# A two-block transformer kernel on one core: other reading places for the modulation sums, later gates, vectors turned in one go

## What is computed

```python
# first block
f = swiglu(rmsnorm(x, ffn1_pre_g), w_gate, w_up, w_down); x = x + 0.5*rmsnorm(f, ffn1_post_g)
# mixer: one projection h @ w_in is split into q, k, v of 12 attention heads,
#   q, k, v, o of 4 mLSTM heads, 4 + 4 gate columns (i_pre, f_pre) and two branch gates
ig = i_pre + i_bias;  lf = log_sigmoid(f_pre + f_bias)      # mLSTM gates, per head and token
att = dilated_window_attention(...);  hm = mlstm_chunkwise(q, k, v, ig, lf)
merged = sigmoid(g_a)*(att @ w_att_branch) + sigmoid(g_m)*(ml @ w_mlstm_branch)
x = x + rmsnorm(merged @ w_out, mix_post_g)
x = x + 0.5*rmsnorm(swiglu(...), ffn2_post_g)
# second block, two layers (i = 0: sparse attention, i = 1: short convolution)
mod = silu(c) @ ada_w[i] + ada_b[i]                          # 1024 -> 6144, one row
sh1, sc1, g1, sh2, sc2, g2 = split(mod, 6)
h = rmsnorm(x, norm1_g[i])*(1 + sc1) + sh1;  x = x + g1*mixer_i(h)
h = rmsnorm(x, norm2_g[i])*(1 + sc2) + sh2;  x = x + g2*swiglu(h, ...)
```

## Time and profile before

| | |
|---|---|
| median of three runs | 2851.05 us |
| the profiled execution, its own time | 2849.39 us |
| its span | 2847.6 us |
| PE busy | 2756.6 us, 97% of the span |
| DVE, ACT, POOL busy | 48%, 33%, 29% |
| mean granted PE clock | 0.97 of full speed |

### The profile page before, as it was taken

One profiled execution on the slowest core, in us unless ns is written; L12 is line 12 of the kernel. 1 busy time (PEld: TensorE's weight loads), 2 busy tenths in 40 slices (PEclk: granted clock), 3 DMA queues, 4 the chain that ended last, 5 costly groups with the idle time before them and its releaser, 6 DMA issues.

```text
span 2847.6 us, 30406 instructions
## 1 busy us (share of the span) xinstructions
PE 2756.6 (97%) x12474; PEld 2174.6 (76%) x12474; DVE 1359.3 (48%) x1932; ACT 936.6 (33%) x1528; POOL 813.4 (29%) x683
## 2 busy tenths in 40 slices
PE   7999998999999989999999987999999999999999
PEld 6788886777777768888888654468888888888887
DVE  4343255545665534544424697564333454633323
ACT  4222243333444322432224423443222232332221
POOL 5563024443654487457300233410000000000000
PEclk9999999999999999999999996699999999999999
DMA  5453243333333255344433211022333423333332
GB/s 168 141 148 121 97 114 107 101 95 87 110 104 104 82 144 163 115 134 148 119 126 101 62 45 44 9 67 67 96 97 133 126 59 96 126 97 96 96 111 82
DMA packets 380765, 294.52 MB, mean 103 GB/s; under 512 B 14805, under 2 KB 334545, under 8 KB 380625
## 3 DMA queue, kind: packets, MB, share of 16 engines
q1 hardware_dynamic: 363632, 240.33, 28.4%
q0 software_dynamic: 16992, 52.25, 6.1%
HBM read 290.40 MB, written 2.13 MB: 103 GB/s over the span
## 4 chain that ended last, share of the span: by engine, by line
PE 84%; DVE 9%; ACT 3%; POOL 2%; DMA 1%; issue 1%; SPq 0%; DVEq 0%; ACTq 0%; POOLq 0%
PE PS L342 17%; PE PS L343 16%; PE PS L345 14%; PE PS L408 7%; PE PS L410 7%; PE PS L409 7%; PE PS L347 2%; PE PS L839 2%; PE PS L379 1%; PE PS L380 1%; PE PS L381 1%; PE PS L860 1%; DVE SCW L2076 1%; DVE M L2073 1%; PE PS L849 1%; DVE WL L1474 1%
## 5 line engine op out<-in xcount | busy, mean ns | idle before, releaser
L342 PE MATMUL PS<-HH,WH 128*128 128x512 f32 x2248 | 906.6, 403 | 0.0
L343 PE MATMUL PS<-HL,WH 128*128 128x512 f32 x2248 | 878.6, 391 | 0.0
L345 PE MATMUL PS<-HH,WL 128*128 128x512 f32 x1967 | 769.7, 391 | 0.0
L1474 DVE TENSOR_TENSOR WL<-RAW,WH 128x1024 fp32r<-128x1024 f32 (+1 forms) x306 | 400.9, 1312 | 546.1 <-ACT WH L899 545.9
L342 PEld LDWEIGHTS PS<-HH,WH 128*128 128x128 f32 x2248 | 424.6, 189 | 131.2 <-issue 47.5
L343 PEld LDWEIGHTS PS<-HL,WH 128*128 128x128 f32 x2248 | 424.5, 189 | 90.8 <-issue 6.8
L899 ACT ACTIVATE WH<-RAW 128x1024 fp32r<-128x1024 f32 (+1 forms) x318 | 330.5, 1041 | 377.4 <-PE PS L347 312.5
L345 PEld LDWEIGHTS PS<-HH,WL 128*128 128x128 f32 x1967 | 371.0, 189 | 79.4
L2248 POOL TENSOR_SCALAR ADA<-ADA,CA 128x512 f32<-128x512 f32 x168 | 294.7, 1754 | 12.5 <-DMA ADA<-in_ada_w 5.0
L2245 POOL TENSOR_TENSOR ASUM<-ASUM,ADA 128x512 f32<-128x512 f32 x168 | 230.4, 1372 | 14.0
L1474 DVE TENSOR_TENSOR WLr<-RAWD,WHr 128x1024 fp32r<-128x1024 f32 x82 | 101.7, 1240 | 257.4 <-ACT WHr L899 257.4
(11 more groups left out here) (327 smaller groups left out, 3468.4 us busy)
## 6 DMA issues: line engine op xcount, KB each, us to landing
ADA<-in_ada_w POOLq DMA_DIRECT2D x192, 256.0 KB, 3.2
RAW<-in_ffn_w_gate SPq DMA_DIRECT2D x88, 512.0 KB, 3.9
RAW<-in_ffn_w_up SPq DMA_DIRECT2D x88, 512.0 KB, 3.9
RAWD<-in_ffn_w_down SPq DMA_DIRECT2D x88, 512.0 KB, 3.4
RAW<-in_w_in SPq DMA_DIRECT2D x84, 512.0 KB, 3.9
RAW<-in_conv_w_in SPq DMA_DIRECT2D x24, 512.0 KB, 3.9
RAW<-in_attn_w_in SPq DMA_DIRECT2D x16, 512.0 KB, 3.8
RAW<-in_w_mlstm_branch SPq DMA_DIRECT2D x8, 512.0 KB, 4.0
```

What stands on the lines that cost most here:

```text
L342: pe.matmul(PS[:, b, :], wh[:, k, :], hi[:, k, :], start=k == 0, stop=False)
L343: pe.matmul(PS[:, b, :], wh[:, k, :], lo[:, k, :], start=False, stop=False)
L345: pe.matmul(PS[:, b, :], wl[:, k, :], hi[:, k, :], start=False, stop=False)
L1474: return v.tensor_tensor(out, x, y, op).then_inc(*tick("dve", *event))
```

## The change

Three edits. The list `FLUSH` still holds 24 chunks; its first 15 are the same (up to chunk 135). Before, entries 15 to 18 were chunks 142, 149, 156 and 163, and 19 to 23 were 178, 185, 192, 199 and 206. Now entries 15 to 17 are 144, 153 and 160, and 18 to 23 are 178, 185, 192, 199, 206 and 213. On all three engines `gates()` is appended when chunk `MIX` + 4 (the fifth of the mixer) has been handled, and not stepped at once. The three later groups of vectors are turned by three transposes in a row and copied by one instruction.

```diff
-FLUSH = (list(range(F1 + 8, F1 + 40, 7)) + list(range(MIX + 6, BR2 + 13, 7)) + list(range(F2 + 3, F2 + 40, 7)))[:24]
+FLUSH = (list(range(F1 + 8, F1 + 40, 7)) + list(range(MIX + 6, BR1 + 1, 7)) + [BR1 + 9, BR2 + 2, BR2 + 9]
+         + list(range(F2 + 3, F2 + 40, 7)))
...
 # tensor_program
     def later_vectors():
         for g in range(1, 4):
-            turn_vectors(g)
+            w.wait_ge(*at("vs", g))
+        for g in range(1, 4):
+            c0, n = SIZES[g]
+            ins = pe.transpose(PS[:, 7, c0:c0 + n], m["VS"][0:n, g, :], C[0:n, C_ID:C_ID + n])
+        ins.then_inc(*tick("pe", "vt", 3))
+        free[7] = ("vec", 3)
...
                 i = MIX + 1 + 9 * hd + 3 * g + which
                 if i >= at_i["chunk"]:
                     fm(h, side_bank())
+                if i == MIX + 4:
+                    behind.work.append(gates())
...
     head(1, [4, 0, 1])
     w.wait_ge(*at("c2"))
-    behind.work.append(gates())
-    behind.step()
...
 # vector_program (the gates' edit is the same there and in scalar_program)
     def later_vectors():
-        for g in range(1, 4):
-            turn_vectors(g)
+        c0, c1 = SIZES[1][0], sum(SIZES[3])
+        w.wait_ge(*at("vt", 3))
+        copy(VT[:, c0:c1], PS[:, 7, c0:c1], "vec", 3)
```

## The result

The changed kernel takes 2824.24 us (median of 4 runs, 2823.04 to 2825.23), the kernel before on the same chip 2851.91 us (2851.04 to 2853.88): ratio 0.9909, 95% interval 0.9896 to 0.9922. Forecast were 2830.0 us and faster. The direction is right, and the gain of 27.7 us is 6.7 us larger than the 21.0 us of the sum. The profiled execution of after has 2824.99 us.

The account below looks back on a forecast made before the run. PE was taken as the bound, busy 2756.6 of 2847.6 us. Gains of 3.1 + 4.0 + 13.9 = 21.0 us gave a profiled 2828.4 us and a median of 2830.0 us, range 2825 to 2836 us for 8 in 10.

Parts of the forecast that it names:

- the sum: Whole kernel: gains of 3.1 for vectors, 4.0 for gates and 13.9 for reads, together 21.0 us.
- The bound: PE, busy 2756.6 of 2847.6 us, bounds both sides of each place, so a microsecond won there should reach the end.
- Edit 1: Later vectors, before the next projection: three transposes in a row replace waits for DVE's copies; gain 3.1 us, bounds 2.9 to 3.3.
- Edit 2: Gates in the mixer: 9.8 us of wait and slow clock before, gain 4.0 us, bounds -3.8 to 9.8.
- The walk: Gates' order of work on PE, ACT and DVE: two PE waits for ACT's copies remain, 1.9 and 2.9 us.
- The clock loss: Gates: the second wait, 2.9 us, may bring PE's clock down; half of a 2 us loss counted, 1.0 us.
- The rival with two falls of the clock: Gates: both waits bring the clock down, the gates' edit gives 0; gain 17.0, 2834.0 us; chance 0.13.
- The rival in which the waits vanish: Gates: both waits disappear, one rope less standing ahead of the scans; gain 26.8, 2824.2 us; chance 0.08.
- The table loads: ACT at the gates: 1.28 us each without drain; the skill's extra 1380 ns would lengthen the first wait by 2.8 us.
- Edit 3: Reads of the modulation sums in the branches: two waits and slow clock go; gain 13.9 us, bounds 0 to 14.5.
- the readiness walk: POOL begins each sum after the previous read; sums 16 and 17 ready 5 us or more and 2.2 us before their reads.
- The rival of POOL as the limit: Second FFN: POOL's time per sum exceeds the 39 us between reads; 10 us slower, 2861 us; chance 0.03.

Follow-up runs that it names:

- 3.5 alone: Kernel before with only the three later vector groups turned by transposes in a row and copied by one instruction; 2841.79 us, ratio 0.9974.
- 12.0 alone: Kernel before with only the new reading places of the sums in `FLUSH`; 2833.31 us, ratio 0.9946.
- the first read moved alone: Kernel before with sum 15 read two chunks later, other reads as before, the next still forced at the first branch's end; 2852.32 us, ratio 1.0013.
- both runs with POOL's wait: POOL's subtraction of one chunk held until DVE's add: on the kernel before 2848.03 us; on the changed kernel with gates' bias adds earlier, last Exp later 2819.44 us.

## Why the prediction was right

- **The bound.** PE is the bound on both sides of each place, so what is won there reaches the end. It did: the leads that arise at 281, 482 and 1148 us stand at 1610 us, less the 0.9 of the read that moved.
- **Edit 1.** Forecast 3.1 (2.9 to 3.3), measured 3.3 in after and 3.5 alone. PE goes on 0.20 us after the three transposes begin, not 0.35.
- **Edit 2.** Forecast 4.0, measured 4.8 at its place. The walk found both waits and their releasers. The first was 2.20 for 1.9; the second 1.02 for 2.9. It is smaller since DVE's scans came 0.8 us earlier (448.48 for 449.3), and since PE, at half clock behind the first wait, came to it 1.1 us later (452.5 for 451.4). The clock loss, counted as half of 2 us behind the second wait, came behind the first: 1.6 us. (The prediction prices one such fall at 2, 2.5 and 3.4 us in different places.) So the term was 0.8 too small, with its two parts off in opposite ways. Another 1.5 us near 795 us appear with this edit, by chance of the clock, and no step of mine had them. The rival with two falls of the clock did not come true. The rival in which the waits vanish named 2824.2 us, the very median that was measured, and is wrong all the same: both waits are there, and went only where the bias adds and the Exp were moved.
- **The table loads.** 439.70 + 1.28 is 440.98, and the next activation starts at 441.00; no drain again. The Trainium skill (ScalarE: Activation LUTs, What ACT_TABLE_LOAD costs) adds some 1380 ns to each switch, by which, as an estimate, the first wait would have been 2.20 + 2 x 1.38, some 5 us. The rows decided rightly.
- **Edit 3.** Forecast 13.9, measured 13.3 in after (14.3 less 0.9) and 12.0 alone. The 0.9 are the read that moved; the prediction said that the reads stay, only elsewhere. The term that was off is the time at which sum 17 is ready: I had it 2.2 us ahead of its read, and PE waits 0.81 us. From read 16 to sum 17 POOL took 40.1 us (1060.23 to 1100.37) and not 36.9. 2.6 of these 3.2 us pass before POOL begins: DVE's copy of sum 16 starts 3.0 us behind the read and not 1.9, since a low part stands ahead of it, and the row's transfer holds POOL for 2.27 us and not 0.71. POOL's timeline of after, then of before:

```profile
1067.52 2.31 POOL L2255 TENSOR_SCALAR ASUM<-ADA,CA 128x512 f32<-128x512 f32 x1 [2.27 <-DMA mod_rows<-ASUM]
```

```profile
1061.42 1.56 POOL L2248 TENSOR_SCALAR ASUM<-ADA,CA 128x512 f32<-128x512 f32 x1 [0.71 <-DMA mod_rows<-ASUM]
```

The argument that the sums depend on each other, which the readiness walk used, is confirmed by the first read moved alone: 33.7 us to the next sum, forecast 34.6.
- **The rival of POOL as the limit** did not come true. In the second FFN POOL's timeline of after, which answers to the earlier trace rows, still waits ahead of each row that it sends, at least the 3.73 us of this one:

```profile
1363.09 0.54 POOL L2290 DMA_DIRECT2D mod_rows<-ASUM  x1 [3.73 <-DVE ASUM L1492]
```

- **What the sum did not have.** 6.7 us, of which 0.4 are in the three terms. The rest is the 3.7 of the sparse layer (1.6 lost to the clock, 5.3 won where a long add and a wait are gone), the 1.5 near 795 us, -0.4 behind the sparse layer and +0.3 in it beside that, -2.1 in the first 30 us, and 3.3 by which the profiled executions differ from their medians: 0.4 + 3.7 + 1.5 - 0.1 - 2.1 + 3.3 = 6.7. The range of 2825 to 2836 us took the doubt from the three edits alone and left all of this out; the median lies 0.8 us under it. So the three places and their sizes came out by the argument; that the total, with parts of both signs beside it, stayed near the forecast was luck.

## What to carry to other kernels

A wait that PE has for a copy on an engine that works in order belongs to what stands ahead of the copy there. Ask of each such operation who needs it soon, and put those that nobody needs behind the copy: that gave 5.2 us here on top of the change, with no work removed. Waits for the results of one producer that works on them in turn are a chain; to price them singly, by the idle time in front of each, gave 4.5 + 2.1 for the first of them and the run -3.3. And a shift of everything by some microseconds dissolves and makes long operations and falls of the clock worth 1 to 5 us each, so a range for a sum of terms should be wider than the terms' own bounds by about that. Last, a wait that is added to test a collision tests it only if the trace shows the engine standing at it; in both runs with POOL's wait it did not, and the numbers came out as the theory had them all the same.

## What the runs showed of the hardware

- Where a two-input subtraction on POOL (128 x 1024, 2.38 us) starts 0.03 to 0.06 us ahead of a two-input add on DVE (128 x 128), the add takes 2.47 to 2.49 us; where it starts 1.2 us or more behind the add's end, 0.29. So it is in four and ten traces; no run changed their order by an edit.
- PE's granted clock stays at 0.50 for over 50 us in which PE counts as busy 20 of 20 us, under matmuls of 64 rows and few columns, and comes back at moments that differ by 24 and 34 us between executions of the same instructions. One unread matmul of 128 x 256 with each of 24 scores went with an early return in all four executions, and the lead still grew by 2.4 us.
- A wait of 2.2 us cost 1.6 us of clock behind it, one of 1.02 us nothing; twenty matmuls of one column with no wait at all were followed by a fall worth 0.9 to 1.7 us at one to three of four like places in every trace.
